# One more shift section summed on VectorE, and the second attention's links and weight splits in another order

## The reference, cut to what matters

```python
ua = jnp.einsum('bse,ed->bsd', ya * jax.nn.silu(ga), w_up_a[l])   # ub, uc likewise
gates = jax.nn.sigmoid(gm.reshape(B, S, N_BRANCH, D))
merged = gates[:, :, 0] * ua + gates[:, :, 1] * ub + gates[:, :, 2] * uc
x = x + jnp.einsum('bsd,de->bse', merged, w_o[l])
```

```python
mod = silu_c @ ada_w[layer] + ada_b[layer]
shift_m, scale_m, gate_m, shift_f, scale_f, gate_f = jnp.split(mod, 6, axis=-1)
h = modulate(rms_norm_2(x, norm_mix_w[layer]), shift_m, scale_m)
y, y_ctx = even_mixer(h, h_ctx, w_in, w_out, rpb, lb, hg_norm_w, ...)  # attention and recurrence
x = x + gate_m[:, None, :] * y
h = modulate(rms_norm_2(x, norm_ffn_w[layer]), shift_f, scale_f)
x = x + gate_f[:, None, :] * conv_ffn(h, ...)
```

## Time and profile before

| | before |
|---|---|
| median of 3 runs | 1071.91 us (1070.92 to 1072.86) |
| the profiled execution's own time | 1072.09 us |
| its span in the profile | 1069.5 us |
| TensorE matmul busy | 1047.1 us, 98% |
| VectorE busy | 780.1 us, 73% |
| ScalarE busy | 580.8 us, 54% |
| GpSimd busy | 66.7 us, 6% |
| bytes moved by DMA | 220.29 MB |

### The profile page before, as it was taken

The page is one execution under the profiler, slowest core; times in us unless marked ns, Lnnn a source line. Parts: engine busy times, 40 slices in busy tenths (PEclk is TensorE's granted clock), DMA queues, the critical chain, the costliest instruction groups (busy, mean ns, idle before and its releaser), DMA issues.

```text
span 1069.5 us, 21436 instructions
## 1 busy us (share of the span) xinstructions
PE 1047.1 (98%) x9044; PEld 999.7 (93%) x9044; DVE 780.1 (73%) x1128; ACT 580.8 (54%) x883; POOL 66.7 (6%) x78
## 2 busy tenths in 40 slices
PE   8999999999999999999999999999999999999997
PEld 8989889999999999897688999999999999999996
DVE  6367778765576768987877999977687769677642
ACT  5456665565445675534656655533554457565432
POOL 2000000000010514000101000000010020000000
PEclk9999999999999999999999999999999999999999
DMA  9557656565755684444557888767768766555621
GB/s 283 175 182 255 223 172 213 181 198 181 243 169 161 190 224 157 132 145 157 200 183 251 275 288 274 268 250 290 261 224 284 227 213 208 187 182 179 236 79 40
DMA packets 165916, 220.29 MB, mean 206 GB/s; under 512 B 4498, under 2 KB 146222, under 8 KB 165821
## 3 DMA queue, kind: packets, MB, share of 16 engines
q1 hardware_dynamic: 164442, 215.67, 61.3%
q0 software_dynamic: 832, 1.65, 0.8%
q10 hardware_dynamic: 546, 1.60, 0.4%
HBM read 217.80 MB, written 1.11 MB: 205 GB/s over the span
## 4 chain that ended last, share of the span: by engine, by line
PE 78%; DVE 15%; ACT 3%; issue 2%; DMA 1%; SPq 0%; DVEq 0%; ACTq 0%
PE psG L577 19%; PE psG L579 18%; PE psG L578 18%; DVE wlo L1841 5%; PE psS L577 4%; PE psS L579 4%; PE psS L578 4%; DVE arow L1905 1%; PE psG L698 1%; PE psG L700 1%; DVE sq L2295 1%; PE psG L711 1%; DVE stat L2343 1%; PE psS L856 1%; PE psG L725 1%
## 5 line engine op out<-in xcount | busy, mean ns | idle before, releaser
L1841 DVE TENSOR_TENSOR wlo<-raw,whi 128x1024 fp32r<-128x1024 f32 x311 | 376.7, 1248 | 102.0 <-ACT whi L1252 96.7
L577 PE MATMUL psG<-Hlo,whi 128*128 128x256 f32 x1420 | 404.6, 285 | 2.5 <-DVE wlo L1841 1.4
L579 PE MATMUL psG<-Hhi,whi 128*128 128x256 f32 x1420 | 400.1, 282 | 0.0
L578 PE MATMUL psG<-Hhi,wlo 128*128 128x256 f32 x1420 | 399.9, 282 | 0.0
L1252 ACT CAST whi<-raw 128x1024 fp32r<-128x1024 f32 x311 | 314.2, 1047 | 117.5 <-PE psG L579 30.5
L577 PEld LDWEIGHTS psG<-Hlo,whi 128*128 128x128 f32 x1420 | 268.3, 189 | 6.4 <-issue 4.1
L578 PEld LDWEIGHTS psG<-Hhi,wlo 128*128 128x128 f32 x1420 | 268.4, 189 | 0.0
L579 PEld LDWEIGHTS psG<-Hhi,whi 128*128 128x128 f32 x1420 | 268.4, 189 | 0.0
L577 PE MATMUL psS<-Glo,whi 128*128 128x256 f32 x316 | 89.8, 284 | 0.0
L579 PE MATMUL psS<-Ghi,whi 128*128 128x256 f32 x316 | 89.1, 282 | 0.0
L578 PE MATMUL psS<-Ghi,wlo 128*128 128x256 f32 x316 | 89.1, 282 | 0.0
(11 more groups left out here) (452 smaller groups left out, 1780.8 us busy)
## 6 DMA issues: line engine op xcount, KB each, us to landing
raw<-in_ada_w_dram SPq DMA_DIRECT2D x48, 1024.0 KB, 5.6
raw<-in_ffn_w_up_dram SPq DMA_DIRECT2D x44, 1024.0 KB, 5.3
raw<-in_w_in_dram SPq DMA_DIRECT2D x29, 1024.0 KB, 6.5
raw<-in_ev_w_in_dram SPq DMA_DIRECT2D x26, 1024.0 KB, 5.5
raw<-in_ffn_w_down_dram SPq DMA_DIRECT2D x22, 1024.0 KB, 4.9
raw<-in_od_w_in_dram SPq DMA_DIRECT2D x12, 1024.0 KB, 8.1
raw<-in_w_in_dram SPq DMA_DIRECT2D x9, 512.0 KB, 6.7
raw<-in_w_o_dram SPq DMA_DIRECT2D x4, 1024.0 KB, 5.2
```

What stands on the lines that cost most here:

```text
L577: mm(o, a_hi, b_lo, start=first, stop=False, skip_group_check=shared)
L578: mm(o, a_lo, b_hi, start=False, stop=False, skip_group_check=shared)
L579: return mm(o, a_hi, b_hi, start=False, stop=last, skip_group_check=shared)
L1841: V.tensor_tensor(ring_half(wlo, v, h - H0[v]), src, ring_half(whi, v, h - H0[v]).bitcast(F32), ALU.subtract).then_inc(lo_split, 1)
```

## The change

Section 3 goes from TensorE to VectorE: its four units now stand in the gate stage, after branch c of i = 1, b of 2, a and c of 3. Section 4 and half of section 11 move to earlier places, so six units are left at the attention's places. `spread(3)` and `sum_ada(3)` stand between the output projections. In the attention `scale_output` goes from VectorE to ScalarE (one instruction of 128x1024 becomes eight of 128x128), weighing piece 0 comes a step later, before the turn of piece 2, and the splits of evoB, evoA and the first feed-forward weights stand at other, mostly earlier, points of ScalarE's and VectorE's order.

```diff
-ON_VECTOR = (2, 5, 6, 7, 8, 9)
+ON_VECTOR = (2, 3, 5, 6, 7, 8, 9)
...
-              2: ("slot8", "slot9", "slot10", "slot11"), 3: ("hg7a", "hg7b", "na0a", "na1a"),
-              4: ("na2a", "na3a", "na4a", "na4b"), 7: ("up0.9", "up0.10", "fd0.0", "fd0.2"),
+              2: ("slot8", "slot9", "slot10", "slot11"), 3: ("gu1c", "gu2b", "gu3a", "gu3c"),
+              4: ("hg7a", "na0a", "na1a", "na1b"), 7: ("up0.9", "up0.10", "fd0.0", "fd0.2"),
...
-              9: ("od0", "od1", "od2", "od3"), 11: ("na8b", "na9a", "tail2a", "tail2b")}
+              9: ("od0", "od1", "od2", "od3"), 11: ("na4a", "na9a", "tail2a", "tail2b")}
...
@@ plan_units, gate stage @@
             section(f"up_{br}{i}", "U" if br != "b" else "V", f"w_up_{br}", i * 256, 1)
+            ada(f"gu{i}{br}")
@@ TensorE, output projections @@
             for n, u in enumerate(SPAN["wo"]):
                 project(u, Whi, Wlo, ready=(merge_ready, 0) if n == 0 else None)
+                if n == 0:
+                    pe.wait_ge(turned_kept, 8)
+                    spread(3)
+                elif n == 2:
+                    sum_ada(3)
@@ TensorE, attention @@
+                if s == 4:
+                    na_weigh(0)
                 if 2 <= s < NA + 2:
                     na_turn(s - 2, 0)
...
-                if s >= 3:
+                if s >= 4:
                     na_weigh(s - 3)
...
                 if n == 0:
                     pe.wait_ge(pT_kept, NT0 + 2 * NA)
-                    sum_ada(3)
-                elif n == 1:
                     sum_ada(4)
@@ ScalarE, attention @@
+            def scale_output():
+                act.wait_ge(sub_inv, 2)
+                o = ot.rearrange("p t j v -> p (t j) v")
+                for n in range(8):
+                    ins = nc.scalar.activation(o[:, n, :], o[:, n, :], ACT.Copy, scale=lbc[:, 2, n:n + 1])
+                ins.then_inc(hg_gated, 1)
...
-                if s == 4:
-                    ahead(SPAN["hg"][1])
...
                 elif s == 3:
                     act.wait_ge(sub_taken, 3)
                     nc.scalar.copy(Hhi[:, 4:6, :], lg[:, 0, 0:2, :])
+                    ahead(SPAN["hg"][1])
...
+                if s == 1:
+                    scale_output()
+                elif s in (5, 6, 7):
+                    ahead(SPAN["evoB"][s - 5])
                 if s < NA:
                     exps(NG + s, ...)
+                if s >= NA:
+                    split_through(SPAN["evoA"][1 + s - NA])
                 if s in EVO_AT:
-                    ahead(SPAN["evoB"][EVO_AT[s]])
                     keep_turned(s - 2, 1)
...
             for n, u in enumerate(SPAN["evoA"]):
                 if n:
                     square_part("ffn0", n - 1)
-                if n in (1, 2):
-                    split_through(SPAN["fa0.0"][0], (2, 1)[n - 1])
-                else:
-                    ahead(u)
+                split_through(SPAN["fv0.0"][0], 1 if n else 2)
@@ VectorE, gate stage @@
+                    if b < 2:
+                        add_rows(f"gu{i}{br}")
...
                 split_value(merged[:, :, :], Whi[:, 2 * i:2 * i + 2, :], Wlo[:, 2 * i:2 * i + 2, :],
                             merge_ready, i + 1)
+                add_rows(f"gu{i}c")
@@ VectorE, attention: keep_na is cut in two, its split_value is now split_na @@
             for s in range(NA + 4):
+                j = (s - 5) // 2
+                kept_now = s >= 5 and s % 2 == 1
                 if s < NA:
                     bias_near(s)
                 if s == 3:
                     norm_output(1)
-                if s >= 5 and s % 2 == 1:
-                    keep_na((s - 5) // 2)
-                if s - 1 in EVO_AT:
+                if s == NA + 1:
+                    add_gated(SPAN["evoB"][3], 3, 0, 2, ready=False)
+                if kept_now:
+                    keep_na(j)
+                if s - 1 in EVO_AT and s <= NA:
                     add_gated(SPAN["evoB"][EVO_AT[s - 1]], EVO_AT[s - 1], 0, 2, ready=False)
+                if s in (5, 7):
+                    ahead(SPAN["evoB"][s - 5])
                 if 1 <= s <= NA:
                     normalise_near(s - 1)
-                if s == 1:
-                    scale_output()
-                elif s == 2:
+                if s == 2:
                     norm_output(0)
+                elif s == 3:
+                    ahead(SPAN["hg"][1])
                 elif s == 4:
-                    ahead(SPAN["hg"][1])
                     dve.wait_ge(hg_high, 1)
...
-                if s in EVO_AT:
-                    ahead(SPAN["evoB"][EVO_AT[s]])
+                elif s == 6:
+                    ahead(SPAN["evoB"][1])
+                if kept_now:
+                    split_na(j)
+                if NA <= s <= NA + 2:
+                    split_through(SPAN["evoA"][1 + s - NA])
             for n, u in enumerate(SPAN["evoA"]):
                 if n == 0:
-                    ahead(u)
+                    split_through(SPAN["fv0.0"][0], 1)
...
-                if n == 3:
-                    ahead(u)
-                elif n:
-                    split_through(SPAN["fa0.0"][0], (2, 1)[n - 1])
+                if n:
+                    split_through(SPAN["fv0.0"][0], 1)
@@ GpSimd @@
-            for n in (3, 4):
-                fold_row(n)
+            fold_row(4)
```

More of the change, by code:

```diff
@@ L401, in ada_row @@
         def ada_row(n):
-            if n == 3:
+            if n == 4:
                 return qke[:, 1, :, :].rearrange("p h s -> p (h s)")
-            return arow0[:, n % 2, :] if n < 3 else arow1[:, ROW[n], :]
-        ROW = {4: 0, 7: 0, 5: 2, 6: 3, 10: 4, 8: 5, 9: 0, 11: 1}
+            return arow0[:, n % 2, :] if n < 4 else arow1[:, ROW[n], :]
+        ROW = {7: 0, 5: 2, 6: 3, 10: 4, 8: 5, 9: 0, 11: 1}
         def output_bank(n):
@@ L949, in turn_ctx_keys @@
                     pe.wait_ge(rms_inv, F["mix0"] + 1)
+                    pe.wait_ge(ada_kept, SUM_IX[3] + 1)
                 for j in range(4):
@@ L1515, in _ @@
                 nc.scalar.copy(Hhi[:, 2 * n:2 * n + 2, :], cxT[:, 2 * n:2 * n + 2, :]).then_inc(vhi_set, 2)
+                if n == 1:
+                    keep_spread(3)
             for g in range(4):
@@ L2166, in _ @@
                 ahead(u)
+                if i == 1:
+                    keep_ada(SUM_IX[3] + 1)
                 if i >= 2:
@@ L2208, in keep_na, with split_na @@
                 then(V.tensor_copy(vt[:, 1, :], psY[:, 0:S]), y_kept, NG + j + 1)
+            def split_na(j):
                 split_value(vt[:, 1, :], Hhi[:, j, :], Hlo[:, j, :], M_ready, 3 + j + 1)
@@ L2317, in _ @@
             keep_o(7)
-            def scale_output():
-                dve.wait_ge(sub_inv, 2)
-                o = ot.rearrange("p t j v -> p (t j) v")
-                r = lbc[:, 2, :].rearrange("p (a b) -> p a b", b=1).to_broadcast([P, 8, P])
-                then(V.tensor_tensor(o, o, r, ALU.mult), hg_gated, 1)
             def norm_output(i):
@@ L2386, in _ @@
                 if n == 0:
-                    keep_ada(SUM_IX[3] + 1)
-                elif n == 1:
                     keep_ada(SUM_IX[4] + 1)
```

## The result

The changed kernel takes **1076.28 us** (median of 5 runs, 1074.96 to 1079.35) against 1071.91 before: 1.0048 of it, with a 95% interval of 1.0037 to 1.0058. That is 0.5% slower, more than the 0.2% that this kernel's measurement can tell, and 2.5 us above the predicted range. (Its own time is only 3.3 us longer than that of the execution profiled before, since 1.7 us of it lie around the span, not 2.6.)

What follows compares the result with a forecast made beforehand. It took TensorE, busy 98% of the span, as the bound, with VectorE setting the pace at the second attention's start. Attention -3.5 us and gate stage +2.45 gave about -1.0, so 1071.0 us, range 1067.8 to 1073.8.

Steps and rivals of the forecast that it cites:

- the last term of the gate stage: Gate stage: section 3's four 1 MB loads take slots, costed at nothing; the whole stage was put at +2.45 us.
- Rival C: Gate stage costs more, VectorE's slack or a load being short: one further place +1.65 us, two +4.3; chance 0.10.
- up_a2 and wo1: Gate stage: TensorE waits for splits standing behind VectorE's sums, +0.85 us at up_a2 and +0.65 at wo1.
- Spread and sum: Gate stage: the spread and sum_ada(3) as added work of TensorE, +0.94 us.
- The wait at evoA0: Attention's end: the last attention value stands behind evoA3's load, so evoA0's fourth tile waits, +2.7 us.
- The attention: Whole attention up to the sum of squares: -1.4 - 1.25 - 1.85 + 2.7 - 1.65 = -3.5 us.
- rival D: Attention gains less because ScalarE takes VectorE's place: evoB0 0.7 us later, sum -0.3; chance 0.03.
- The wait of 1.9 us at the turn of piece 0: Attention before evoB0: ScalarE keeps piece 0 later, so its second half's turn waits some 1.9 us on TensorE.
- The clock: Fall to 1.2 GHz behind evoA0's wait, through the fourth tile and evoA1, 3.65 us more; part of rival B.
- rival B: Slower: evoA0's wait outweighs the attention's gain; +1.0 us with 5.7 us landing, +4.6 with the clock's fall (1075.6); chance 0.15.
- Rival A: Gate stage hides all but the spread, or evoA3 lands soon: both waits small -3.1 us, one -2.2; chance 0.30.

Runs made afterwards that it cites:

- early_add: Changed kernel with VectorE's sums of gu1c, gu2b and gu3a ahead of that branch's product instead of behind it; 1073.00 us.
- evoA3_later: Changed kernel with VectorE's split of evoA3 behind the last attention value instead of ahead of it; 1074.78 us.
- slot_free: Changed kernel with section 11's second unit at na4b instead of na9a, out of evoA3's load slot; 1075.56 us.
- scale_on_vector: early_and_free with the scaling of the recurrence's output back on VectorE, one instruction instead of eight on ScalarE; 1072.54 us.
- gate_only: Kernel before with only the gate-stage part: section 3 on VectorE, its four units gone from the attention; 1077.88 us.
- both_fillers: Changed kernel with five unneeded matmuls each ahead of gm_b3 and of evoA0's fourth tile; 1075.90 us.
- early_and_free: Changed kernel with gu2b and gu3a sums ahead of products, next splits ahead of gu1c and gu3c sums, section 11's second unit at na4b; 1074.47 us.
- attention_only: Changed kernel's attention order with section 3 back on TensorE and all ten units at their old places; 1073.05 us.
- early_free_scale: Changed kernel with the edits of early_add, slot_free and scale_on_vector together; 1068.65 us.
- filler: attention_only with six unneeded matmuls in evoA0, just ahead of the wait for the last attention value; 1070.45 us.

## Why the prediction was wrong

**The step that failed** is the last term of the gate stage: "The four loads of 1 MB take slots [...] I cost them at nothing." It cost 4.98 - 0.85 = 4.1 us up to wo0 (in early_add, which only frees three slots sooner, wo0 starts 0.82 us later than before, and that is the wait at up_a2). I had seen that a load waits for VectorE's sum and judged it by its own due time, "due 9 us later or more". Two things were wrong with that. The load that hurt is not the next one but the third behind it: a queue held for some 10 us lets 3 MB go together, and a landing of 5 to 6.5 us becomes 11.2. And the one who needs it first is not TensorE but ScalarE, whose sigmoid for an earlier projection stands behind the split; TensorE's own need came within 0.2 us of it. Rival C had the direction ("one of the four loads [...] is a microsecond or two less than I think", +1.65 us or +4.3 with two places), with 0.10 of the chances; its +4.3 is close to what came by luck, since it was made of two places at VectorE's full 2.65 us each, and its stated ground against, the distance of the next splits, was the same mistake.

**up_a2 and wo1** held. I had +0.85 us at up_a2: its bracket is 0.77 and its start 1.0 us later than the earlier trace rows. I had +0.65 at wo1: its bracket is 0.35, some 0.3 less. Spread and sum were 0.94 us by the sum; from wo0 to hg7a there are 1.67 us, of which 0.35 is the bracket, 0.94 these two, and 0.4 us stand in no bracket.

**The wait at evoA0** came where and how it was said: 2.12 us against 2.7, with a landing of 3.4 against 3.7 us. evoA3_later and slot_free confirm its cause, and that only about 1 us of the wait itself can be had back, since the next one stands close behind.

**The attention** gave 2.49 us against 3.5. Of the difference 0.7 us is rival D: the scaling takes 0.30 us for each of the eight, my upper end (measured 0.8 in scale_on_vector). Another 1.26 is the clock's fall behind evoA0, and the wait itself was 0.6 shorter than I had it. 3.5 - 0.7 - 1.26 + 0.6 = 2.1, within 0.4 us of it. The wait of 1.9 us at the turn of piece 0 was foreseen and is 1.86; evoB0 waits 0.30 us.

**The clock** I had only inside rival B, at 0.10. It fell twice. In the gate stage this cost nothing, since TensorE would have waited for wo0 anyway (gate_only, both_fillers); in the attention 1.26 us, where rival B had 3.65. I had taken the slow clock to last through the fourth tile and all of evoA1; it was over at 563.3. The Trainium skill's rule was right in direction, and should have had more than a tenth.

**Rival A** fell: of the gate stage's two waits only 0.4 us were hidden beyond the sums, and evoA3's landing was 0.3 us shorter. **Rival B** had the wrong share: its place cost 2.12 + 1.26 us and the attention still gained. Its sum has a slip: +4.6 us on the time before is 1076.5, not 1075.6. That this lies near the measured 1076.28 is luck, since the landing of 5.7 us behind it did not come.

What stays open: why an execution of the same gate stage starts wo0 between 297.17 and 299.23 (the spread is there already when up_a3's load goes, at 263.69 to 265.45, so it comes from ahead of gm_b3); and what decides whether the clock falls. At the turn of piece 0 TensorE waits 1.86 or 1.87 us in six of these kernels: the clock fell there in early_add, evoA3_later and slot_free, and not in the changed kernel, early_and_free and both_fillers.

## What to carry to other kernels

Moving a weight's reader to an engine with idle time also moves the moment at which its buffer comes free. Follow that moment through the load queue, count the bytes that then go together, and find the first engine that needs one of them, with everything that stands behind this need in its order. A summation that nobody waits for still has a due time: that of its slot; placed ahead of the products the sums cost 0.8 us up to wo0, placed behind them 5.0. And a wait of TensorE of about 2 us may be followed by a slow clock, which cost 1.3 to 1.5 us more here, unless the time up to the next wait is slack anyway.

## What the runs showed of the hardware

- The granted clock of TensorE fell to 1.2 GHz close behind waits of 1.97 and 2.12 us (changed kernel), 2.95 (scale_on_vector), 3.26 (attention_only) and 3.85 us (early_and_free). It stayed full behind waits of 2.10 (evoA3_later) and 2.31 us (early_add), and behind 1.87 us it fell in early_add, evoA3_later and slot_free and not in early_and_free and both_fillers, so the length of the wait alone doesn't decide it. In early_add it fell inside the wait. In early_free_scale, whose longest wait in these stages is 1.17 us, it did not fall there.
- Unneeded matmuls in such a wait kept the clock and made a kernel 1.3 us shorter by its span (filler, 1068.7 us against 1070.0 in attention_only).
- The landing of one 1 MB load went from 5.1 us (issued 2.3 us behind 0.5 MB) to 11.2 when it was issued third in 3 MB, 1.3 us behind the first, while a load of 512 KB issued first still took 3.4 us.
- ScalarE's scaling of 128x128 with a factor of its own for each row took 0.30 us each, eight one behind the other 2.45 us, although its activation of the same size that stands in the earlier trace rows had a successor 0.22 us after its start.
